# Four engines' call lists in a new order, six more warm-up matmuls, and seven small constant loads packed into one

## What is computed

```
def reference(x, norm_gain, w_in, q_norm_gain, k_norm_gain, sink_logits, ret_norm_gain, w_out):
    b, s, _ = x.shape
    for _layer in range(DEPTH):
        h = rms_norm(x, norm_gain)
        proj = jnp.einsum('bsd,de->bse', h, w_in)
        aq, ak, av, ag, rq, rk, rv, rg = jnp.split(proj, SPLIT_POINTS, axis=-1)
        attn = window_attention(
...
        ret = retention(
...
        mixed = jnp.concatenate([attn * jax.nn.silu(ag), ret * jax.nn.silu(rg)], axis=-1)
        x = x + jnp.einsum('bse,ed->bsd', mixed, w_out).astype(x.dtype)
    return x
```

## Time and profile before

| what | value |
|---|---|
| time, median of 3 runs | 1569.11 us (1569.06 to 1569.93) |
| profiled execution: time, span from first to last instruction | 1569.28 us, 1567.5 us |
| PE busy | 1555.1 us, 99% of the span, 8132 matmuls |
| DVE, ACT, POOL busy | 1109.5 us (71%), 835.6 us (53%), 379.1 us (24%) |
| mean granted clock of TensorE | 0.998 |

### The profile page before, as it was taken

How to read it: one execution, slowest core, us unless ns; L and a number is a source line. 1 busy time by engine, 2 the same in 40 slices (tenths; PEclk the granted TensorE clock), 3 DMA queues, 4 the chain that set the end, 5 groups by cost and what they waited for, 6 DMA issues and landing times.

```text
span 1567.5 us, 24792 instructions
## 1 busy us (share of the span) xinstructions
PE 1555.1 (99%) x8132; PEld 1358.3 (87%) x8132; DVE 1109.5 (71%) x2899; ACT 835.6 (53%) x2332; POOL 379.1 (24%) x365
## 2 busy tenths in 40 slices
PE   8999999999999999999999999999999999999999
PEld 7798888988889888898988989889898898988887
DVE  6888687787956767576875756857687574775864
ACT  6775665755535455464644645545463454635641
POOL 4554546451212011111101111121120211201200
PEclk9999999999999999999999999999999999999999
DMA  8888486656775354463565644526547455344451
GB/s 314 318 292 306 168 322 233 246 202 231 283 250 220 136 191 179 152 247 122 204 216 196 247 151 175 220 85 247 183 150 276 147 203 191 140 189 134 172 214 54
DMA packets 122639, 321.56 MB, mean 205 GB/s; under 512 B 17680, under 2 KB 59024, under 8 KB 122512
## 3 DMA queue, kind: packets, MB, share of 16 engines
q1 hardware_dynamic: 121552, 318.40, 55.5%
q10 hardware_dynamic: 960, 1.57, 0.3%
HBM read 248.63 MB, written 71.30 MB: 204 GB/s over the span
## 4 chain that ended last, share of the span: by engine, by line
PE 92%; DVE 3%; ACT 1%; DMA 1%; issue 1%; SPq 1%; POOL 0%; ACTq 0%; DVEq 0%; POOLq 0%
PE jb L1408 26%; PE jb L1410 26%; PE jb L1409 26%; PE s L1443 2%; PE ob L1467 2%; PE ptb L1452 2%; PE ob L1427 1%; PE s L1506 1%; PE ab L1517 1%; PE s L1505 1%; DMA stage<-wp_dram 1%; PE s L1344 1%; SPq L362 0%; PE s L1346 0%; PE s L1507 0%
## 5 line engine op out<-in xcount | busy, mean ns | idle before, releaser
L1408 PE MATMUL jb<-wH,hTH 128*128 128x512 f32 (+1 forms) x1024 | 375.2, 366 | 5.7 <-DVE hTL L1146 4.5
L1410 PE MATMUL jb<-wH,hTL 128*128 128x512 f32 (+1 forms) x1024 | 372.0, 363 | 0.0
L1409 PE MATMUL jb<-wL,hTH 128*128 128x512 f32 (+1 forms) x1024 | 371.9, 363 | 0.0
L1408 PEld LDWEIGHTS jb<-wH,hTH 128*128 128x128 f32 x1024 | 193.2, 189 | 24.8 <-DVE wL L862 4.9
L1410 PEld LDWEIGHTS jb<-wH,hTL 128*128 128x128 f32 x1024 | 192.9, 188 | 20.5
L1409 PEld LDWEIGHTS jb<-wL,hTH 128*128 128x128 f32 x1024 | 193.2, 189 | 17.8
L1408 PE MATMUL jb<-wH,mxH 128*128 128x512 f32 x512 | 206.5, 403 | 0.0
L1408 PE MATMUL jb<-hTH,wH 128*128 128x512 f32 x512 | 201.0, 393 | 0.0
L1410 PE MATMUL jb<-wH,mxL 128*128 128x512 f32 x512 | 200.6, 392 | 0.0
L1409 PE MATMUL jb<-wL,mxH 128*128 128x512 f32 x512 | 200.3, 391 | 0.0
L1410 PE MATMUL jb<-hTH,wL 128*128 128x512 f32 x512 | 199.7, 390 | 0.0
(11 more groups left out here) (151 smaller groups left out, 3004.6 us busy)
## 6 DMA issues: line engine op xcount, KB each, us to landing
wH<-scrH SPq DMA_DIRECT2D x144, 512.0 KB, 7.3
wL<-scrL SPq DMA_DIRECT2D x144, 512.0 KB, 7.9
stage<-wp_dram SPq DMA_DIRECT2D x48, 512.0 KB, 6.7
scrH<-wH SPq DMA_DIRECT2D x48, 512.0 KB, 6.6
scrL<-wL SPq DMA_DIRECT2D x48, 512.0 KB, 7.3
wH<-scrH SPq DMA_DIRECT2D x48, 384.0 KB, 5.2
wL<-scrL SPq DMA_DIRECT2D x48, 384.0 KB, 6.6
xt<-xT_dram SPq DMA_DIRECT2D x15, 512.0 KB, 6.8
```

The costliest lines, as they stand in the source:

```text
L1408: pe.matmul(o, lh, rh_, start=i == 0, stop=False)
L1409: pe.matmul(o, lh, rl_, start=False, stop=False)
L1410: m = pe.matmul(o, ll, rh_, start=False, stop=i == last)
```

## The change

The calls of POOL, ACT, DVE and PE stand in another order; each engine has the same calls as before, apart from 18 warm-up matmuls in place of 12. The loads of `ngain`, `rgain`, `qkg` (four) and `ident` become one load of a tensor `small`, packed ahead on the host, at the head of SP's queue; the four names are now views of it, and one semaphore stands for them.

```
-WARM = 12
+WARM = 18
+SMALL = KT + RET_HEADS + 2 + P
...
-        rgain = sb("rgain", [P, RET_HEADS])
-        ident = sb("ident", [P, P])
-        ngain = sb("ngain", [P, KT])
-        qkg = sb("qkg", [P, 2])
+        small = sb("small", [P, SMALL])
+        ngain, rgain, qkg, ident = small[:, 0:8], small[:, 8:16], small[:, 16:18], small[:, 18:SMALL]
...
-            sp.dma_start(ngain[:, :], norm_gain.rearrange("(k p) -> p k", p=P), allow_slow_non_contiguous=True
-                         ).then_inc(S["s_gains"], 16)
+            sp.dma_start(small[:, :], small_in).then_inc(S["s_gains"], 16)
...
-            sp.dma_start(ident[:, :], c_ident).then_inc(S["s_ident"], 16)
...
-            xpow(0, 0); wl1(0, 1, 0); wl1(0, 1, 1); xpow(0, 1); wl1(0, 1, 2); rpow(0, 0); wl1(0, 1, 3); xpow(0, 2)
...
+            xpow(0, 0); rpow(0, 0); xpow(0, 1); wl1(0, 1, 0); wl1(0, 1, 1); rpow(0, 1); xpow(0, 2); xpow(0, 3)
+            wl1(0, 1, 2); wl1(0, 1, 3); wl1(0, 1, 4); wl1(0, 1, 5); wl1(0, 1, 6); rpow(0, 2); wl1(0, 1, 7); rpow(0, 3)
```

More of the change, by code:

```diff
@@ L357, in _ @@
             first_rows(3)
[L358 to L363, removed]
             attention_constants(0)
@@ new lines, in _ @@
+            xh(0, 3, 0); xsq(0, 2); xh(0, 3, 1); xsq(0, 3); tqh(0, 0); wh1(0, 1, 2); wh1(0, 1, 3); wh1(0, 1, 4)
+            wh1(0, 1, 5); wh1(0, 1, 6); wh1(0, 1, 7); qkv(0, 2); tqh(0, 1); xrb_copy(0); v_shift(0, 1); exps(0, 0)
+            qkv(0, 3); exps(0, 1); ag(0, 0); wh1(0, 2, 0); wh1(0, 2, 1); v_shift(0, 2); v_shift(0, 3); tqh(0, 2)
+            pth(0, 0); wh1(0, 2, 2); ag(0, 1); wh1(0, 2, 3); wh1(0, 2, 4); wh1(0, 2, 5); tqh(0, 3); rqh(0)
+            wh1(0, 2, 6); wh1(0, 2, 7); exps(0, 2); rk(0); wh1(1, 0, 0); obcopy(0, 0); pth(0, 1); wh1(1, 0, 1)
@@ new lines, in _ @@
+            gnx(2, 1); rvg(2, 3); wh1(2, 3, 0); kwh_ah(2, 3); ocopy(2, 2); mth(2, 0); rh(2, 3); wh1(2, 3, 1)
+            wh1(2, 3, 2); wh1(2, 3, 3); wh1(2, 3, 4); wh1(2, 3, 5); qkv(3, 0); gnx(2, 2); wh1(2, 3, 6); qkv(3, 1)
+            wh1(2, 3, 7); tqh(3, 0); mth(2, 1); ocopy(2, 3); v_shift(3, 0); rh(3, 0); qkv(3, 2); tqh(3, 1); mth(2, 2)
+            v_shift(3, 1); exps(3, 0); qkv(3, 3); gnx(2, 3); wh1(3, 1, 0); tqh(3, 2); pth(3, 0); mth(2, 3)
+            wh1(3, 1, 1); wh1(3, 1, 2); wh1(3, 1, 3); exps(3, 1); wh1(3, 1, 4); wh1(3, 1, 5); wh1(3, 1, 6)
@@ new lines, in _ @@
+            xh(1, 2, 0); xh(1, 2, 1); kwh_ah(3, 2); ocopy(3, 1); rh(3, 2); rvg(3, 3); gnx(3, 1); kwh_ah(3, 3)
+            ocopy(3, 2); rh(3, 3); xh(1, 3, 0); mth(3, 0); xh(1, 3, 1); wh1(3, 3, 0); wh1(3, 3, 1); wh1(3, 3, 2)
+            qkv(4, 0); wh1(3, 3, 3); wh1(3, 3, 4); wh1(3, 3, 5); gnx(3, 2); qkv(4, 1); wh1(3, 3, 6); wh1(3, 3, 7)
+            rh(4, 0); v_shift(4, 0); qkv(4, 2); tqh(4, 0); mth(3, 1); ocopy(3, 3); v_shift(4, 1); v_shift(4, 2)
+            qkv(4, 3); tqh(4, 1); mth(3, 2); exps(4, 0); gnx(3, 3); tqh(4, 2); mth(3, 3); exps(4, 1); pth(4, 0)
@@ new lines, in _ @@
+            wl1(0, 0, 5); wl1(0, 0, 6); xl(0, 0, 2); xl(0, 0, 3); xg(0, 1, 0); wl1(0, 0, 7); xg(0, 1, 1); xl(0, 1, 0)
+            xg(0, 2, 0); xms_(0, 0); xl(0, 1, 1); xl(0, 2, 0); xg(0, 2, 1); qk_stats(0, 0); v_parts(0, 0); xl(0, 2, 1)
+            xms_(0, 1); qk_norm(0, 0); xg(0, 3, 0); xg(0, 3, 1); qk_stats(0, 1); xl(0, 3, 0); xl(0, 3, 1); xms_(0, 2)
+            xms_(0, 3); carry_in(0); qk_norm(0, 1); tql(0, 0); v_parts(0, 1); part1(0, 0); tql(0, 1); qk_stats(0, 2)
+            part1(0, 1); qk_stats(0, 3); qk_norm(0, 2); part2(0, 0); qk_norm(0, 3); agz(0, 0); part2(0, 1); agg(0, 0)
@@ new lines, in _ @@
+            v_parts(0, 2); v_parts(0, 3); agz(0, 1); tql(0, 2); ptl(0, 0); agg(0, 1); rq_decay(0); part1(0, 2)
+            tql(0, 3); carry_out(0); part2(0, 2); part1(0, 3); mix(0, 0); ptl(0, 1); part2(0, 3); kw_am(0, 0)
+            rvg(0, 0); mix(0, 1); kwl_al(0, 0); kw_am(0, 1); ptl(0, 2); rupd(0, 0); rvg(0, 1); gna(0, 0); kwl_al(0, 1)
+            rl(0, 1); kw_am(0, 2); gnv(0, 0); carry_in(1); gnm(0, 0); gnb(0, 0); rvg(0, 2); mix(0, 2); rupd(0, 1)
+            ptl(0, 3); gna(0, 1); kwl_al(0, 2); rl(0, 2); kw_am(0, 3); gnv(0, 1); gnm(0, 1); rvg(0, 3); rupd(0, 2)
@@ new lines, in _ @@
+            mix(0, 3); kwl_al(0, 3); rl(0, 3); gna(0, 2); mtl(0, 0); gnv(0, 2); qk_stats(1, 0); gnb(0, 1)
+            wl1(0, 3, 2); gnm(0, 2); wl1(0, 3, 3); v_parts(1, 0); qk_norm(1, 0); qk_stats(1, 1); gnb(0, 2)
+            wl1(0, 3, 6); wl1(0, 3, 7); qk_norm(1, 1); v_parts(1, 1); rupd(0, 3); qk_stats(1, 2); v_parts(1, 2)
+            tql(1, 0); mtl(0, 1); gna(0, 3); gnv(0, 3); qk_norm(1, 2); rl(1, 0); xms_(1, 0); gnm(0, 3); mtl(0, 2)
+            part1(1, 0); tql(1, 1); add(0, 0); gnb(0, 3); qk_stats(1, 3); add(0, 1); xms_(1, 1); part1(1, 1)
@@ new lines, in _ @@
+            qk_norm(2, 2); qk_stats(2, 3); gnb(1, 3); add(1, 0); part1(2, 1); ptl(2, 0); add(1, 1); xms_(1, 3)
+            part2(2, 1); add(1, 2); qk_norm(2, 3); add(1, 3); tql(2, 2); mtl(1, 3); v_parts(2, 2); add(1, 4)
+            part1(2, 2); add(1, 5); v_parts(2, 3); part2(2, 2); tql(2, 3); add(1, 6); carry_out(2); add(1, 7)
+            part1(2, 3); ptl(2, 1); part2(2, 3); agz(2, 0); agg(2, 0); agz(2, 1); agg(2, 1); mix(2, 0); rq_decay(2)
+            mix(2, 1); ptl(2, 2); mix(2, 2); ptl(2, 3); kw_am(2, 0); rvg(2, 0); kwl_al(2, 0); carry_in(3); mix(2, 3)
@@ new lines, in _ @@
+            rupd(3, 2); kwl_al(3, 3); gna(3, 2); rl(3, 3); gnb(3, 1); mtl(3, 0); xl(1, 3, 0); gnv(3, 2)
+            qk_stats(4, 0); xl(1, 3, 1); wl1(3, 3, 2); gnm(3, 2); wl1(3, 3, 3); qk_norm(4, 0); qk_stats(4, 1)
+            gnb(3, 2); rupd(3, 3); v_parts(4, 0); wl1(3, 3, 6); qk_norm(4, 1); wl1(3, 3, 7); v_parts(4, 1); rl(4, 0)
+            qk_stats(4, 2); v_parts(4, 2); tql(4, 0); mtl(3, 1); gna(3, 3); qk_norm(4, 2); gnv(3, 3); part1(4, 0)
+            tql(4, 1); gnm(3, 3); mtl(3, 2); add(3, 0); part2(4, 0); gnb(3, 3); qk_stats(4, 3); part1(4, 1); tql(4, 2)
@@ new lines, in _ @@
+            add(12, 1); tql(13, 2); add(12, 2); add(12, 3); part1(13, 2); tql(13, 3); add(12, 4); carry_out(13)
+            part2(13, 2); add(12, 5); part1(13, 3); ptl(13, 1); add(12, 6); part2(13, 3); add(12, 7); agz(13, 0)
+            agg(13, 0); agz(13, 1); agg(13, 1); mix(13, 0); rq_decay(13); ptl(13, 2); mix(13, 1); kw_am(13, 0)
+            rvg(13, 0); kwl_al(13, 0); mix(13, 2); ptl(13, 3); carry_in(14); kw_am(13, 1); rvg(13, 1); mix(13, 3)
+            rupd(13, 0); kwl_al(13, 1); gna(13, 0); kw_am(13, 2); rl(13, 1); gnv(13, 0); gnm(13, 0); rvg(13, 2)
@@ new lines, in _ @@
+            qk_norm(14, 2); add(13, 0); qk_stats(14, 3); v_parts(14, 2); v_parts(14, 3); part2(14, 1); ptl(14, 0)
+            qk_norm(14, 3); add(13, 1); tql(14, 2); add(13, 2); add(13, 3); part1(14, 2); tql(14, 3); add(13, 4)
+            carry_out(14); part2(14, 2); add(13, 5); part1(14, 3); ptl(14, 1); add(13, 6); part2(14, 3); add(13, 7)
+            agz(14, 0); agg(14, 0); agz(14, 1); agg(14, 1); mix(14, 0); rq_decay(14); ptl(14, 2); mix(14, 1)
+            kw_am(14, 0); rvg(14, 0); kwl_al(14, 0); mix(14, 2); ptl(14, 3); carry_in(15); kw_am(14, 1); rvg(14, 1)
```

849 lines of the change are left out of this document (401 added, 448 removed).

## The result

The changed kernel takes **1599.83 us** (median of 3, 1597.82 to 1600.57) against 1569.11 before: a ratio of 1.0193, 95% interval 1.0179 to 1.0208, 30.7 us slower. The prediction, 1569.8 us with a range up to 1573.2, is wrong. The profiled execution took 1599.83 us, with a span of 1597.9 us and a mean clock of 0.998.

The account below looks back on a forecast made before the run. PE was taken as the bound, busy 1364.29 of 1365.00 us from 200 us on. Terms +2.6 (PE behind after S_(0,1)), -1.9 and 0 gave +0.7 us on 1569.28: 1570.0, as a median 1569.8; range 1563.8 to 1573.2.

Parts of the forecast that it names:

- First job: Start of the kernel: first job begins at about 8.9 us, job(0,1) at about 15.4 against 17.40, -2.0 us.
- Jobs 1 to 3: Unit 0 on PE: the 1.2 us wait goes, job(0,3) ends at about 29.6, PE 2.0 us ahead.
- S_(0,1) has lost its cover: Unit 0, behind job(0,3): PE waits 4.6 us at S_(0,1), until 35.3, going from 2.0 us ahead to 2.6 behind.
- R2: Slower rival: the clock falls in the wait at S_(0,1), 2.4 us more, +3.1 in all, 1572.3 us; chance 0.17.
- Later waits of before: 1.9 gone: After 31.34 us, TQ and S_ of units 0 and 1: 1.9 of 2.1 us of short idle time goes.
- Units 2 to 15 ... every small call finds its inputs ready: Late units: small calls never wait, the tightest inputs 0.3 to 0.5 us early; 0 us, bounds -2 and +1.7.
- R3: Slower rival: A(n,2) waits 0.69 us for DVE in each of 11 late units, 7.6 us, 1577 us; chance 0.05.
- The neighbours on PE: Units 2 to 15: a pair of small calls costs 0.09 us more; 19 more pairs, +1.7 us at most.
- The bound: From 200 to 1565 us PE is busy 1364.29 of 1365.00 us; no order of other engines gains over 0.7 us.

Follow-up runs that it names:

- slower_fill: Changed kernel with every POOL subtraction wl1 replaced by a fill with zeros in sixteen pieces: 1587.24 us.
- late_carry: Changed kernel with carry_in(n) on DVE moved back to just ahead of tql(n,0), units 1 to 15: 1592.69 us.
- vshift_behind_tqh: Changed kernel with v_shift(n,0) on ACT moved behind qkv(n,1) and tqh(n,0) in nine late units: 1589.67 us.
- three_earlier: Changed kernel with the moves of vshift_behind_tqh, late_carry and s01_and_low_part together: 1578.49 us.
- old_lists: Changed kernel with the four call lists of before, keeping the one load of constants and the 18 warm-up matmuls: 1566.85 us.
- s01_behind_job: Changed kernel with S_(0,1) moved behind job(0,4) on PE: 1600.34 us.
- late_cover: Changed kernel with PE's order changed in nine late units: job(n,3) ahead of TQ(n,1), S_(n,0) and MT(n-1,3), the next job ahead of S_(n,1): 1619.18 us.
- old_lists_two_moves: Old lists with the one load and 18 warm-up matmuls, and on PE I(1,0) behind job(1,10), I(0,2) behind job(1,2): 1573.06 us.
- s01_and_low_part: Changed kernel with S_(0,1) behind job(0,4) on PE and wl1(0,1,7) ahead of rpow(0,2) on POOL: 1595.57 us.
- late_vshift: Changed kernel with v_shift(n,0) on ACT moved behind qkv(n,1) in nine late units: 1597.59 us.
- old_lists_rvg: Old lists with the one load and 18 warm-up matmuls, and on ACT rvg(1,0) ahead of wh1(2,0,5) and wh1(2,0,6): 1565.24 us.

## Why the prediction was wrong

**First job: right.** It began at 8.77 (8.9 forecast), `job(0,1)` at 15.82 (15.4), and the clock stayed at 1.00. The warm-up was costed too long, 18 matmuls in 6.08 us in place of 7.4; so PE stood 1.2 us ahead of the job, without harm.

**Jobs 1 to 3: half right.** `carry_in` held nothing up, but ahead of `job(0,3)` PE still waited 1.5 us for the last `hTL` (before, 1.2). The job ended at 30.5 (29.6 forecast), and PE was 1.1 us ahead in place of 2.0.

**S_(0,1) has lost its cover: right, and R2 with it.** The wait was 4.9 us (4.6 forecast) and ended at 36.81 (35.3, with 36.1 as the late bound): `part1(0,0)` began at 31.63 in place of 30.4, since S_(0,0) came that much later, and `d` in it took 1.12 us. The clock fell behind it as R2 had it, for 2.9 us of loss against 2.4 forecast. With both, PE was about 7 us behind (2.6 forecast, 1.5 from the later end of the wait, 2.9 from the clock), where R2 had 5.0.

**"Later waits of before: 1.9 gone" failed.** They did not go, they grew, and so in units 2 and 3, which the next step has at 0: S_(1,2), S_(2,2) and S_(3,3) wait 1.4 us each or less, A(1,2) and A(2,2) 2.3 and 2.2, beside smaller ones. From 100 to 200 us PE was busy 95.61 us (before 99.36), from 200 to 400 us 193.82 (before 200.00). Two things stand in neither step at a price. Behind S_(0,1) I costed every DVE operation at its free duration, though the earlier trace rows show the hold; slower_fill puts its price at 12.6 us at most in all, some 10 by the estimate above. And `carry_in(n+1)` has no price, though it ends a transfer: late_carry puts that at 5 to 7 us.

**"Units 2 to 15 ... every small call finds its inputs ready" failed.** The walk of a late unit, which the prediction does not print, gave TQ(n,1) as ready in time. It took `qkv(n,1)` as starting when `job(n,1)` ends and left out that ACT stands in turn at `v_shift(n,0)`, which waits for DVE's `v_parts(n,0)`, now behind `qk_norm(n,0)`. In unit 9 the inputs of TQ(n,1) take 6.0 us from the end of `job(n,1)` at 897.8 to 903.8, and PE has 5.0 us of work in between, to 902.8. From 400 to 1500 us PE was busy 1091.93 us in the changed kernel and 1100.00 before; vshift_behind_tqh gives back 7.6 of these 8.1 us (10.2 by the medians). With units 2 and 3 the term, at 0 with bounds of -2 and +1.7, lost 14.2 us from 200 to 1500 us, and of the whole sum it was off most.

**R3** had the right kind of loss, a wait in each late unit, at the wrong call, and a chance of 0.05. The neighbours on PE, which I priced, were a small matter: from XB(2) to XB(3), four units with hardly a wait of PE in either, the kernel before took 385.4 us and vshift_behind_tqh, with the new order of PE, 386.4.

**The bound was read as one-sided.** "No order can take more than 0.7 us out of it" says what there is to gain; the same row, PE never waiting, also says that every input comes in time by margins that the new lists are free to use up.

The Trainium skill, page "SBUF — State Buffer", section "SBUF: two separate sides", says that a VectorE operation with two inputs in SBUF meets the lock only against a GpSimd operation that reads SBUF. The subtractions and the fills agree: `d` took 1.22 us beside subtractions and 0.16 without, `v_parts` 1.28 beside subtractions and 0.21 beside fills, which read nothing. The power function, which reads SBUF too, does not agree, as the prediction found (L991 took 0.69 us inside one).

What stays open: the waits left in three_earlier, 11.6 us above old_lists, were not taken apart, and the split of the holds over the places was not measured.

## What to carry to other kernels

A kernel whose bounding engine hardly ever waits has little to gain and much to lose by a new order of the others, so walk every small call of a steady unit with the waits of the engines in between, above all calls that stand in line for a transfer or for another engine. Written-out lists of several engines are one schedule: here, moving a call later on the bounding engine alone passed its wait on each time (s01_behind_job, late_cover, old_lists_two_moves) and gave nothing or cost time, while making its input earlier gave time back clear of the spread in late_carry, vshift_behind_tqh and s01_and_low_part, and these gains added up. Those of late_vshift and old_lists_rvg lie within the spread.

## What the runs showed of the hardware

- A load of 0.5 KB of sinks took 5.29 us from issue to landing, and DVE stood 4.7 us for it.
- Behind a wait of 4.9 us the clock fell in each of the executions profiled with it; behind the wait at A(1,2) it fell in some (a wait of 2.4 us and a granted clock of 0.83 from 182 to 192 us in late_vshift) and not in others (2.3 us and 1.00 in the changed kernel).
- SP's 7.01 us in one issue were gone once the seven small loads were one: the sinks were issued at 13.09 us in the changed kernel and at 22.68 before.
